# Second rotary table by a selection matmul, reordered per-layer embedding stages, and moved panel splits in a two-block decoder kernel

## What is computed

```python
x = x + rms_norm(y, post_norm_g[i])
x = x + (p[i] @ ple_w_proj[i]) * jax.nn.sigmoid(x @ ple_w_gate[i])
```

## Time and profile before

| | us |
|---|---|
| median of 3 runs | 2409.71 (2407.66 to 2410.79) |
| the profiled execution | 2407.74 |
| its span in the trace | 2405.9 |
| PE busy | 2221.8 |
| DVE busy | 1145.5 |
| POOL busy | 923.7 |
| ACT busy | 860.5 |

### The profile page before, as it was taken

The page is one execution under the profiler, slowest core; times in us unless marked ns, Lnnn a source line. Parts: engine busy times, 40 slices in busy tenths (PEclk is TensorE's granted clock), DMA queues, the critical chain, the costliest instruction groups (busy, mean ns, idle before and its releaser), DMA issues.

```text
span 2405.9 us, 28934 instructions
## 1 busy us (share of the span) xinstructions
PE 2221.8 (92%) x10318; PEld 1832.4 (76%) x10318; DVE 1145.5 (48%) x1728; ACT 860.5 (36%) x1253; POOL 923.7 (38%) x704
## 2 busy tenths in 40 slices
PE   4899999878899999988999999998999998999996
PEld 3778888656788888866777788887788876888885
DVE  7445353684666666666245322223454455322224
ACT  3333233434444444344343322323244424322222
POOL 2434444333433433323443445453333231454542
PEclk9999999999999999989999999999999999999998
DMA  4222322222221122221321222224221111322221
GB/s 140 85 78 70 109 74 87 83 75 101 71 87 70 70 80 77 71 95 71 105 76 64 88 102 90 102 90 122 70 71 61 62 53 35 104 90 103 87 105 53
DMA packets 37833, 200.15 MB, mean 83 GB/s; under 512 B 4331, under 2 KB 9579, under 8 KB 15372
## 3 DMA queue, kind: packets, MB, share of 16 engines
q1 hardware_dynamic: 28496, 188.76, 22.3%
q10 hardware_dynamic: 9276, 10.57, 1.5%
HBM read 194.07 MB, written 5.24 MB: 83 GB/s over the span
## 4 chain that ended last, share of the span: by engine, by line
PE 77%; DVE 11%; ACT 4%; DVEq 2%; issue 2%; POOL 2%; DMA 0%; ACTq 0%; POOLq 0%
PE bank L376 26%; PE bank L377 25%; PE bank L378 25%; POOL WL L339 2%; ACT WH L916 2%; DVE ACC L1503 1%; DVE PKL L1441 1%; DVE HL L1463 1%; DVE SS L1468 1%; DVE R L1586 1%; ACT HH L970 1%; DVE MYL L1441 0%; DVE T L1644 0%; DVE RS L1457 0%; DVE R L1457 0%
## 5 line engine op out<-in xcount | busy, mean ns | idle before, releaser
L339 POOL TENSOR_TENSOR WL<-RAW,WH 128x512 fp32r<-128x512 f32 x700 | 923.5, 1350 | 1448.6 <-ACT WH L916 1448.6
L376 PE MATMUL bank<-HH,WH 128*128 128x512 f32 x1320 | 528.0, 400 | 60.2 <-POOL WL L339 16.5
L377 PE MATMUL bank<-HL,WH 128*128 128x512 f32 x1320 | 520.4, 394 | 0.0
L378 PE MATMUL bank<-HH,WL 128*128 128x512 f32 x1320 | 519.6, 394 | 0.0
L916 ACT ACTIVATE WH<-RAW 128x2048 fp32r<-128x2048 f32 x175 | 334.0, 1909 | 439.7 <-PE bank L378 439.1
L376 PEld LDWEIGHTS bank<-HH,WH 128*128 128x128 f32 x1320 | 251.7, 191 | 123.5 <-issue 30.0
L378 PEld LDWEIGHTS bank<-HH,WL 128*128 128x128 f32 x1320 | 251.7, 191 | 53.7
L377 PEld LDWEIGHTS bank<-HL,WH 128*128 128x128 f32 x1320 | 252.0, 191 | 52.0 <-issue 1.0
L376 PE MATMUL bank<-HIDH,WH 128*128 128x512 f32 x512 | 200.6, 392 | 5.1 <-POOL WL L339 5.1
L377 PE MATMUL bank<-HIDL,WH 128*128 128x512 f32 x512 | 200.1, 391 | 0.0
L378 PE MATMUL bank<-HIDH,WL 128*128 128x512 f32 x512 | 200.1, 391 | 0.0
(11 more groups left out here) (363 smaller groups left out, 3817.1 us busy)
## 6 DMA issues: line engine op xcount, KB each, us to landing
RAW<-panels SPq DMA_DIRECT2D x175, 1024.0 KB, 4.7
X<-xin SPq DMA_DIRECT2D x4, 512.0 KB, 7.0
xsave<-X ACTq DMA_DIRECT2D x4, 512.0 KB, 2.8
X<-xsave ACTq DMA_DIRECT2D x1, 2048.0 KB, 8.7
TAB<-scratch ACTq DMA_DIRECT2D x16, 128.0 KB, 3.2
out<-ACC SPq DMA_DIRECT2D x8, 256.0 KB, 2.1
scratch<-O SPq DMA_DIRECT2D x4, 256.0 KB
RS<-decay ACTq DMA_DIRECT2D x4, 256.0 KB, 2.5
```

Of the source, the lines that this page charges most:

```text
L339: end = gp.tensor_tensor(WL[:, s, cs], RAW[:, s, cs], WH[:, s, cs].bitcast(f32), ALU.subtract)
L376: nc.tensor.matmul(o, ah, bh, start=start, stop=False)
L377: nc.tensor.matmul(o, ah, bl, start=False, stop=False)
L378: return nc.tensor.matmul(o, al, bh, start=False, stop=stop)
```

## The change

- Tables: `EVERY4`, a 128x128 selection matrix, is loaded in `per_layer_input(0)`; PE multiplies it with `COS1` and `SIN1` after projection tile 3 (banks 6 and 7), and ACT copies the two banks to `COS2` and `SIN2`. `angles(2, ...)` and two Sin activations go.
- Per-layer input: the root of the post norm stands after projection tile 0; the splits of panels n+1 and n+2 stand among the projection copies and the high halves of x; in `last_out` the running sum lags one tile behind the sum of outputs.
- "Next tile's sum ahead of a low half": wherever DVE adds a result to X and then makes `HL`, it now adds tile f first and makes `HL` of tile f-1 after it. The split behind it stands before `HH[6]` where it stood after `HH[7]`.
- MLA input, gating mixer, feed-forward: splits stand earlier, as the diff shows.
- Banks: the mixer's first value half uses banks 4 to 7, units 0 and 1 of the first pair of the dilated attention use banks 6 and 7, and its units 2 and 3 both run before the first scores.
- End: squares are added as X is finished; ACT multiplies by the gain ahead of the root; DVE multiplies six tiles by the inverse root and POOL two.

```diff
     for n in range(ATT_PAIRS):
-        order.append((n, 0))
         if n > 0:
-            order.append((n - 1, 11))
-        order += [(n, j) for j in range(1, 6)]
+            order += [(n, 0), (n - 1, 11), (n, 1)]
+        order += [(n, j) for j in range(2, 6)]
...
     order.append((ATT_PAIRS - 1, 11))
     banks = {use: i % 2 for i, use in enumerate(order)}
+    banks[0, 0], banks[0, 1] = 6, 7
     banks[ATT_PAIRS - 1, 12], banks[ATT_PAIRS - 1, 13] = 3, 5
...
-            for k in range(KD):
-                sp.wait_ge(S["final_ready"], k + 1)
+            for k in (0, 1, 2, KD - 2, 3, 4, KD - 1, 5):
+                if k < KD - 2:
+                    sp.wait_ge(S["final_ready"], k + 1)
+                else:
+                    sp.wait_ge(S["final_ready_too"], k - KD + 3)
                 sp.dma_start(out[k], ACC[:, k, :]).then_inc(S["out_stored"], 16)
...
+            gp.wait_ge(S["norm_hi"], KD * len(SPLIT) + KD)
+            gp.wait_ge(S["final_inverse"], 1)
+            for k in (KD - 2, KD - 1):
+                gp.tensor_tensor(ACC[:, k, :], ACC[:, k, :], R[:, :], ALU.mult).then_inc(S["final_ready_too"], 1)
...
                     if f == 1:
                         sum_of_squares(f"post{L}")
+                    if L == 0 and f == 3:
+                        pe.wait_ge(S["const_loaded"], 48)
+                        for j, table in enumerate((COS1, SIN1)):
+                            end = nc.tensor.matmul(bank(6 + j)[:, :], EVERY4[:, :], table[:, :], start=True, stop=True)
+                        end.then_inc(S["sines"], 1)
...
-                os_ = [bank(4 * cc + tt) for tt in range(NT)]
+                os_ = [bank(4 * (1 - cc) + tt) for tt in range(NT)]
                 for j in range(2):
...
-                        sum_of_squares("mix0", cols=True)
+                        sum_of_squares("mix0", cols=True, banks=(0, 1))
...
                 unit(n, 2)
+                if n == 0:
+                    unit(n, 3)
                 att_scores(n, 0)
-                unit(n, 3)
+                if n > 0:
+                    unit(n, 3)
                 if n > 0:
...
 
+                if k == KD - 2:
+                    split_at(panel_behind)
                 nc.scalar.activation(HH[:, k, :], src, ACT.Copy, scale=gain(name, k)).then_inc(S["norm_hi"], 1)
-                if k == KD - 1:
-                    split_at(panel_behind)
...
-                squares(f"post{L}", KD, y_made)
-                split_at(n + 1)
-                for f in range(KD):
+                def projected(f):
                     tile_done(act, "ple_proj_made", f, KD, n, base=7 * L)
                     hi(PJ[:, f, :], B[f % 4][:, :]).then_inc(free[f % 4], 1)
-                    if f == 1:
-                        root(f"post{L}", D_MODEL)
-                for k in range(KD):
+
+                def high_x(k):
                     act.wait_ge(S["ple_x_new"], KD * L + k + 1)
                     hi(GH[:, k, :], X[:, k, :]).then_inc(S["ple_hi"], 1)
+
+                squares(f"post{L}", KD, y_made)
+                if L == 0:
+                    act.dma_start(EVERY4[:, :], moves[1]).then_inc(S["const_loaded"], 16)
+                projected(0)
+                root(f"post{L}", D_MODEL)
+                projected(1)
+                projected(2)
+                split_at(n + 1)
+                projected(3)
+                projected(4)
+                for k in range(3):
+                    high_x(k)
+                    projected(5 + k)
+                high_x(3)
+                split_at(n + 2)
+                for k in range(4, KD):
+                    high_x(k)
+                if L == 0:
+                    act.wait_ge(S["sines"], 3)
+                    for j, table in enumerate((COS2, SIN2)):
+                        nc.scalar.activation(table[:, :], B[6 + j][:, :], ACT.Copy).then_inc(free[6 + j], 1)
+                    act.drain().then_inc(S["sines"], 1)
                 for f in range(KD):
-                    if f % 2 == 0:
+                    if f > 0 and f % 2 == 0:
                         split_at(n + 2 + f // 2)
                     tile_done(act, "ple_gate_made", f, 2, n + 1 + f // 2, base=4 * L)
...
             for f in range(KQ + KC):
+                if f % 2 == 0:
+                    split_at(N_MLAIN + 2 + f // 2)
                 act.wait_ge(S["mla_z"], f + 1)
...
                     nc.scalar.activation(CQH[:, f, :], ACC[:, f, :], ACT.Copy, scale=gain("qn", f)).then_inc(S["latent_hi"], 1)
-                if f % 2 == 1:
-                    split_at(N_MLAIN + 2 + f // 2)
-                if f == 3:
-                    for j, dst in enumerate((COS2, SIN2)):
-                        act.wait_ge(S["angle"], j + 3)
-                        nc.scalar.activation(dst[:, :], ACC[:, 6 + j, :], ACT.Sin).then_inc(S["sines"], 1)
             root("cq", Q_LORA, None, True)
...
                     tile_done(act, "mix_v_made", 4 * cc + tt, 4, N_MIX + 2 * cc + 1)
                     act.wait_ge(S["cols_ready"], 1)
-                    nc.scalar.activation(NV[:, tt, 512 * cc:512 * cc + 512], B[4 * cc + tt][:, :], ACT.Gelu,
+                    b = 4 * (1 - cc) + tt
+                    nc.scalar.activation(NV[:, tt, 512 * cc:512 * cc + 512], B[b][:, :], ACT.Gelu,
                                          scale=RC[:, 2 * tt:2 * tt + 1], accum_out=ST[:, cc, tt:tt + 1])\
-                        .then_inc(free[4 * cc + tt], 1)
+                        .then_inc(free[b], 1)
                     act.drain().then_inc(S["mix_gelu"], 1)
-                split_at(N_MIX + 3 + 2 * cc)
+                    if tt == 0:
+                        split_at(N_MIX + 3 + 2 * cc)
...
-                    for j in range(2):
-                        for f in range(2 * j, 2 * j + 2):
-                            act.wait_ge(S["mlp_relu"], c * 4 + (at + f + 1))
-                            nc.scalar.activation(T[:, f, :], TG[:, f % 2, :], ACT.Square).then_inc(S["mlp_hid_f32"], 1)
-                            act.drain()
-                            hi(HIDH[:, f, :], T[:, f, :]).then_inc(S["mlp_hid_hi"], 1)
-                        split_in(c, 4, n0 + 2 + j)
-                        if last and L == 0:
-                            bias_table(2 * j)
-                            bias_table(2 * j + 1)
+                    for f in range(4):
+                        if f in (0, 3):
+                            split_in(c, 4, n0 + 2 + f // 3)
+                        act.wait_ge(S["mlp_relu"], c * 4 + (at + f + 1))
+                        nc.scalar.activation(T[:, f, :], TG[:, f % 2, :], ACT.Square).then_inc(S["mlp_hid_f32"], 1)
+                        act.drain()
+                        hi(HIDH[:, f, :], T[:, f, :]).then_inc(S["mlp_hid_hi"], 1)
+                        if last and L == 0 and f % 2 == 1:
+                            bias_table(f - 1)
+                            bias_table(f)
...
-            squares("final", KD, updated("mlp_done", KD))
+            last_x = updated("x_updated", 3 * KD)
+            for k in range(KD):
+                src = last_x(k)
+                if k >= 3:
+                    act.wait_ge(S["norm_added"], (KD - 1) * FULL.index("final") + k - 2)
+                nc.scalar.activation(SQ[:, k % 2, :] if k > 0 else SS[:, :], src, ACT.Square).then_inc(S["norm_sq"], 1)
+                if k < KD - 1:
+                    nc.scalar.activation(ACC[:, k, :], src, ACT.Copy, scale=gain("final", k)).then_inc(S["norm_hi"], 1)
+            nc.scalar.activation(ACC[:, KD - 1, :], X[:, KD - 1, :], ACT.Copy, scale=gain("final", KD - 1)).then_inc(S["norm_hi"], 1)
             root("final", D_MODEL)
...
+            def add_square(name, k):
+                ve.wait_ge(S["norm_sq"], KD * FULL.index(name) + k + 1)
+                v.tensor_tensor(SS[:, :], SS[:, :], SQ[:, k % 2, :], ALU.add).then_inc(S["norm_added"], 1)
...
                     v.tensor_tensor(ACC[:, f, :], ACC[:, f, :], B[banks[f]][:, :], ALU.add).then_inc(S["y_made"], 1)
                     ve.drain().then_inc(free[banks[f]], 1)
-                    if f > 0:
-                        ve.wait_ge(S["norm_sq"], KD * FULL.index(post) + f + 1)
-                        v.tensor_tensor(SS[:, :], SS[:, :], SQ[:, f % 2, :], ALU.add).then_inc(S["norm_added"], 1)
+                    if f > 1:
+                        add_square(post, f - 1)
+                ve.drain()
+                add_square(post, KD - 1)
                 ve.drain().then_inc(S["norm_squares"], 1)
...
                     v.scalar_tensor_tensor(X[:, f, :], T[:, f % 2, :], 0.5, X[:, f, :], ALU.mult, ALU.add)\
                         .then_inc(S["ple_done"], 1)
-                    gained(pre, f)
-
-                if L == 0:
-                    def first_gates(step):
-                        for f in (2 * step, 2 * step + 1):
-                            gated(f)
-
-                    angles(2, SIN2[:, :].bitcast(i32), FREQ2, [ACC[:, j, :] for j in (0, 1, 6, 7)], first_gates)
```

(37 more changed lines are left out.)

56 lines of the change are left out of this document (28 added, 28 removed).

## The result

| | before | after |
|---|---|---|
| median, us | 2410.25 (2407.66 to 2411.34, 4 runs) | 2344.83 (2343.67 to 2345.06, 4 runs) |
| the profiled execution | 2407.74 | 2343.67 |
| its span | 2405.9 | 2341.9 |
| mean granted clock | 0.972 | 0.980 |

The ratio to the kernel before is 0.9729, 95% interval 0.9712 to 0.9746. The change saves 64.0 us of span where 91.2 were forecast; 2344.83 lies above the range (2306 to 2342).

What follows compares the result with a forecast made beforehand. PE, busy 2221.8 of 2405.9 us, was taken as the bound, its waits also costing clock. Terms summed to 93.7 us, less 2.5 for tight panels: 2316.5 for the profiled execution, median 2318, range 2306 to 2342.

Steps and rivals of the forecast that it cites:

- The panels and the MLA input: Per-layer input 0's panels and MLA input: earlier splits end four losses, 8.5 + 6.9 + 6.0 + 7.7 = 29.1 us gained.
- the second gate panel: Per-layer input 1: the panel wait behind its entry goes, 40.19 less 32.8, 7.4 us gained.
- the mixer's banks: Gating mixer: banks 4 to 7, long free, end the first matmul's 4.7 us wait; 7.7 us gained.
- the first chunk: Feed-forward 0, first chunk: third panel's split ahead of two hidden tiles, ready before 1335.57; 7.5 us gained.
- those for "right": Among them: PE's waits on POOL under 15 us, clock above 0.98, no per-layer-input wait over 1.5 us, attention DVE tile 2.2 to 2.4.
- The signs for "wrong": Waits of 2 to 5 us on POOL in the per-layer inputs, or a DVE tile still at 2.9 us.
- the entry of the per-layer inputs: An earlier running sum on DVE brings the chain to the low parts forward: 5.8 us gained in input 0, 7.2 in 1.
- Attention's entry and feed-forward 1: DVE's tile falls from 2.93 to about 2.3 us: 15.7 us gained in dilated attention, 11.5 in the second feed-forward.
- the term of 4.5: Program's end: fewer additions after the last tile, reciprocal 4 to 5 us earlier, final products at 5.6; 4.5 us gained.
- The mixer: Gating mixer, second value half: the split ahead of three Gelus delays the next u panel, a loss of 2.7 us.
- shorter waits stay: Half of eight tight places keep waits: 2334, or 2342 with a slow DVE chain; chance 0.32 together with clock staying low.
- The slower rival: Feed-forward chunks: ACT stops for a slot ahead of hidden tile 3, making low halves late; 2412 and up, chance 0.02.

## Why the prediction was wrong

*Right.* The reading that PE's chain sets the time, that a wait costs its clock too, and that the gains add up from stage to stage. The panels and the MLA input (30.2 for 29.1), the second gate panel, the mixer's banks, the first chunk. The sign, and that no later wait swallows an earlier gain. DVE's tile at the attention's entry is 2.28. Behind the program's start, the largest wait on POOL is the mixer's u panel (8.3 us where near 7 were forecast).

*The signs.* Three of those for "right" did not come: the waits on POOL are 20.5 us and not under 15, the clock is 0.980 and not above it, and the per-layer inputs keep waits of 3.4 us, where none over 1.5 was to be left. The signs for "wrong" looked for waits on POOL there or a tile still at 2.9; none of them named what happened, waits on DVE.

*The step that failed* is the entry of the per-layer inputs (5.8 and 7.2): "a chain (reciprocal, x, GH, GL) that paces the first gate panel". The start of that chain was right: the reciprocal started at 463.12, which is the forecast 461.9 with the 1.2 us that were lost before. But I costed the chain behind it at the durations of before, 0.75 and 0.69, while in the next paragraph I put POOL's two low halves on top of it ("about 474, and POOL is done by 482"). The term came out at -1.2 and -0.3, 14.5 us short. With POOL nearly taken away 14.6 us come back there.

*The rows were there.* In the prediction I gave POOL "6.50 for four beside DVE" and read it as POOL's trouble alone. The other half is DVE's. The trace of before also has an `HL` of 1.57 and a sum of 1.60 us beside a low half at 1664.53, three tiles ahead of the one of the earlier trace rows, whose `HL` I quoted at 0.75. The Trainium skill (SBUF — State Buffer, "SBUF: two separate sides") says that the pair of ports that DVE and GpSimd share is an exclusive lock, and that a DVE operation with two SBUF inputs and a GpSimd operation that reads SBUF hold it against each other for a whole instruction. I had cited that for the two tiles at the end and for nothing else. The trace agrees: 1.6 us with parts of 512 columns, 2.7 with 1024, and 0.67 for an operation that reads PSUM.

*The same cause, smaller.* Attention's entry and feed-forward 1 (12.1 for 15.7, 9.0 for 11.5): the split ahead of tile 6 put a low half on `HL` 6 and 7 (1.36 and 1.75 us), and 7.4 us came back with POOL's low halves taken away. At the end the term of 4.5 was 2.9: the reciprocal did come 4.9 us earlier than the lead of the line above, but "Six on DVE and two on POOL I take at 5.6" was 6.0 from the reciprocal's end to the last product, and with the stores behind it 10.1 us where before had 8.1; that is the 2.0 that the run with all tiles on DVE gave back, where I thought the two ways nearly even.

*The mixer* (-5.6 for -2.7): the order on ACT was costed right (2.95 us from the Gelus), but DVE's scaling of 0.17 us took 1.10 beside POOL, and the longer wait of 8.27 also cost 1.3 us more clock, which I had left out of this term alone.

*Neither forecast nor explained:* 3.4 us in the attention's pairs and about 2.3 in retention and MLA. The waits there are as long as before, but for 0.3 us at one in the pairs and 0.4 at the program's start; the clock behind them stayed low longer in this execution (in the pairs 1.7 us for 0.1 at the second wait, 2.9 for 1.7 at the third). At the third, a wait of 1.98 us in every kernel, the experiments have 0.1 to 2.9 us. None of the four executions of after is faster than the profiled one, so this is not shown to be a spread of single executions; why the clock stays low at one and not at the other remains open. A gap of 1.18 us at 1655.40 in the kernel after was followed by 1.7 us of low clock too, where I had read from the trace before that gaps up to 1.4 us cost none.

Of the rivals "shorter waits stay" came nearest in time (2334 and 2342), with the wrong mechanism: the waits that stayed are on DVE, not on POOL. The slower rival played no part; HIDL's operations are hit in the chunks (0.86 us on average, before 0.71), and PE does not wait there.

## What to carry to other kernels

When a change moves an operation of POOL, list what DVE runs in that stretch, and price every DVE operation with two SBUF inputs at its own time plus the part of POOL's that it meets (here 0.85 us per operation, 3.5 us per low half); put POOL's work under operations that read PSUM or under a reciprocal. A wait that ends earlier is worth its full length only if the chain behind it runs at the old durations in its new neighbourhood. And parts of such a change support each other: undone alone, two of them cost twice what I had worked out for each, or more.

## What was unexpected of the hardware

Not only operations with two SBUF inputs are hit. A DVE operation with one SBUF input and a scalar took 1.32 us beside POOL at the start of the kernel after and 0.43 alone:

```profile
20.45 12.41 POOL L343 TENSOR_TENSOR WL<-RAW,WH 128x512 fp32r<-128x512 f32 x8 [20.00 <-ACT WH L933]
...
29.02 1.32 DVE L1554 TENSOR_SCALAR ACC<-ACC 128x512 f32<-128x512 f32 x1
...
51.79 0.43 DVE L1554 TENSOR_SCALAR ACC<-ACC 128x512 f32<-128x512 f32 x1
```
The tiny one at 1164.22 took 1.10 for 0.17. A reciprocal of one SBUF input (3.35 us under a low half) was not hit. The Trainium skill (SBUF — State Buffer, "Who interferes with whom") names tensor_scalar and copies among those that can take both port pairs in their fast modes, and so contend; the 0.43 us, against 0.69 for a sum of the same size, agrees with a fast mode. No run here tests this by itself: it is read from single rows of one trace.
